# A two-block decoder layer stack: output weights as 512-row by 512-column blocks, and high and low rows side by side in the gate and up products

## The reference

```python
# first block
h = rms_norm(x, norm_mix)
m = gate_0 * (o_sb @ w_sb) + gate_1 * (o_nsa @ w_nsa) + gate_2 * (o_hgrn @ w_hgrn)   # three kinds of attention
x = x + m @ w_out                                    # <- mixer output, 1024 x 1024
x = x + peer_ffn(rms_norm(x, norm_ffn))              # queries, top-16 of keys, 128 gathered expert rows per token
x = rms_norm(x, norm_final)

# second block, two layers
for layer in range(2):
    x = x + 0.5 * rms_norm(swiglu(rms_norm(x), gate, up, down))      # <- F = 2816
    if layer == 0:
        gate_b, gate_c, u = split(rms_norm(x) @ w_conv_in)
        m = (gate_b * conv3(gate_c * u)) @ w_conv_out                # <- convolution output, 1024 x 1024
    else:
        m = diff_attention(rms_norm(x), k, v)
    x = x + rms_norm(m)
    x = x + 0.5 * rms_norm(swiglu(rms_norm(x), gate, up, down))      # <-
    if layer == 0: k, v = split(rms_norm(x) @ w_kv)

swiglu(h) = (silu(h @ w_gate) * (h @ w_up)) @ w_down
```

## Time and profile before

| | us |
|---|---|
| Median of 3 runs (lowest, highest) | 2050.97 (2048.59, 2053.64) |
| Profiled execution, and its span | 2049.09, 2047.2 |
| TensorE matmul busy | 1875.5 (92%) |
| VectorE busy | 1271.8 (62%) |
| ScalarE busy | 773.6 (38%) |
| POOL busy | 409.6 (20%) |
| Mean granted TensorE clock | 0.962 of full speed |

### The profile page before, as it was taken

The page is one execution under the profiler, slowest core; times in us unless marked ns, Lnnn a source line. Parts: engine busy times, 40 slices in busy tenths (PEclk is TensorE's granted clock), DMA queues, the critical chain, the costliest instruction groups (busy, mean ns, idle before and its releaser), DMA issues.

```text
span 2047.2 us, 30706 instructions
## 1 busy us (share of the span) xinstructions
PE 1875.5 (92%) x11294; PEld 1507.1 (74%) x11294; DVE 1271.8 (62%) x2508; ACT 773.6 (38%) x1293; POOL 409.6 (20%) x523
## 2 busy tenths in 40 slices
PE   7999999987877887878889999999999999899998
PEld 7999899943333333333369999999989999778997
DVE  4546856777777767777654457664455545676444
ACT  4446334222222222222243344453345334565333
POOL 4000000345554655555510000000000000010000
PEclk9989999999888888889999999999999999899999
DMA  8324355599999999999966564645555656424553
GB/s 234 102 66 124 83 155 165 224 417 422 422 422 422 422 421 422 422 422 422 421 221 203 184 205 155 197 163 184 185 171 169 205 184 205 144 93 155 185 185 102
DMA packets 228343, 496.73 MB, mean 243 GB/s; under 512 B 21653, under 2 KB 178470, under 8 KB 195494
## 3 DMA queue, kind: packets, MB, share of 16 engines
q1 hardware_dynamic: 185360, 221.36, 34.3%
q0 software_dynamic: 38224, 273.04, 32.4%
q10 hardware_dynamic: 4678, 1.21, 0.3%
HBM read 494.53 MB, written 1.05 MB: 242 GB/s over the span
## 4 chain that ended last, share of the span: by engine, by line
PE 69%; DMA 15%; DVE 6%; POOL 4%; issue 3%; ACT 2%; DVEq 0%; POOLq 0%; ACTq 0%
PE ps L2186 43%; PE acc L2186 25%; DMA rows_xl<-in_peer_uv,idx_now 14%; POOL rows_lo L726 1%; DMA rows_lo<-in_peer_uv,idx_now 1%; POOL rows_xh L726 1%; DVE lo L1387 1%; DVE arena L1774 0%; DVE arena L1778 0%; DVE arena L1781 0%; POOL idx_now L719 0%; DVE arena L1603 0%; ACT diag L1085 0%; POOL rstd L641 0%; ACT arena L1166 0%
## 5 line engine op out<-in xcount | busy, mean ns | idle before, releaser
L1387 DVE TENSOR_TENSOR lo<-raw,hi 128x2048 fp32r<-128x2048 f32 x198 | 451.6, 2283 | 307.7 <-ACT hi L784 307.6
L2186 PE MATMUL ps<-xh,hi 128*128 128x256 f32 x1840 | 524.9, 285 | 2.6 <-DVE xl L1408 2.1
L2186 PE MATMUL ps<-xl,hi 128*128 128x256 f32 x1840 | 522.5, 284 | 0.0
L2186 PE MATMUL ps<-xh,lo 128*128 128x256 f32 x1840 | 522.4, 284 | 0.0
L784 ACT ACTIVATE hi<-raw 128x2048 fp32r<-128x2048 f32 x198 | 376.4, 1904 | 256.4 <-PE ps L2186 230.4
L2186 PEld LDWEIGHTS ps<-xh,hi 128*128 128x128 f32 x1840 | 354.1, 192 | 6.0 <-issue 4.4
L2186 PEld LDWEIGHTS ps<-xl,hi 128*128 128x128 f32 x1840 | 354.2, 192 | 1.5
L2186 PEld LDWEIGHTS ps<-xh,lo 128*128 128x128 f32 x1840 | 354.1, 192 | 0.1
L636 POOL TENSOR_SCALAR ss<-ss 128x1 f32<-128x1 f32 x28 | 9.4, 337 | 1019.2 <-ACT arena L1166 861.7
L2186 PE MATMUL acc<-rows,diag 128*128 128x512 f32 x192 | 116.9, 773 | 73.8 <-ACT diag L1085 72.0
L2186 PE MATMUL acc<-arena,diag 128*128 128x512 f32 x384 | 172.4, 595 | 6.0 <-ACT diag L1085 5.4
(11 more groups left out here) (420 smaller groups left out, 3308.6 us busy)
## 6 DMA issues: line engine op xcount, KB each, us to landing
raw<-in_w_ffn_gate SPq DMA_DIRECT2D x44, 1024.0 KB, 5.4
raw<-in_w_ffn_down SPq DMA_DIRECT2D x44, 1024.0 KB, 4.9
raw<-in_w_ffn_up SPq DMA_DIRECT2D x41, 1024.0 KB, 5.3
raw<-in_w_in SPq DMA_DIRECT2D x29, 1024.0 KB, 5.4
raw<-in_w_conv_in SPq DMA_DIRECT2D x11, 1024.0 KB, 5.2
raw<-in_w_kv SPq DMA_DIRECT2D x6, 1024.0 KB, 5.4
raw<-in_w_out SPq DMA_DIRECT2D x4, 1024.0 KB, 5.2
raw<-in_w_conv_out SPq DMA_DIRECT2D x4, 1024.0 KB, 7.2
```

What stands on the lines that cost most here:

```text
L1387: v.tensor_tensor(lo[s][:, 0:WORDS[p]], raw[s][:, 0:WORDS[p]], hi[s][:, 0:WORDS[p]].bitcast(F32), ALU.subtract).then_inc(lo_done, 1)
L2186: return nc.tensor.matmul(out, l, r, start=first, stop=last)
```

## The change

1. **Gate and up panels of steps 1 to 10.** `xh` and `xl` become two interleaved views of one buffer, so that the high and low rows of a row block lie side by side. `wide` takes high weights against all 512 columns of a row block in one matmul, and low weights against the 256 high columns. The left half of a bank holds high x high and low x high, the right half high x low. A panel so needs two banks (one for each 128 features): gate in 0 and 1, up in 2 and 3. ScalarE copies the right halves out (`cross`), VectorE adds the left halves to them (`gate_sum`, and the first operation of `product`), SiLU and the product then read and write SBUF. The first wide panels wait for the first step's product, and for its turned rows, between their two halves.
2. **`w_out` and `w_conv_out`.** Each is loaded as four blocks of four row blocks by 512 columns (`quarter`): the upper two first, then the lower two. A tile is 12 matmuls of 512 columns. A bank's sum starts in one panel and ends in another. `project` goes. In the mixer output the third panel's split moves up on ScalarE.

```diff
...
-SUM_STEPS = [1 if n == "pc" else 3 for n, _ in POSTS]
+SUM_STEPS = [2 if n == "pc" else 3 for n, _ in POSTS]
...
-        xh = sb("xh", [P, KD, T], F32R)
-        xl = sb("xl", [P, KD, T], F32R)
+        xboth = sb("xboth", [P, KD, 2, T], F32R)
+        xh, xl = xboth[:, :, 0, :], xboth[:, :, 1, :]
...
+        ff_x = [carve(2, T) for _ in range(2)]
...
+        def quarter(w, j):
+            return w[j // 2 * 512:(j // 2 + 1) * 512, j % 2 * 512:(j % 2 + 1) * 512].rearrange("(k p) n -> p k n", p=P)
...
-                load(p, rows_1024(io["w_out"][0], j * PC))
+                load(p, quarter(io["w_out"][0], j))
...
-            split(FIRST["w_out"] + 2)
+                if n == 0:
+                    split(FIRST["w_out"] + 2)
...
+                def cross(p, up, m=0, r=0):
                     act.wait_ge(panel_used, p + m * r + 1)
-                    act.wait_ge(evacuated, along(EVAC, p, m, r))
-                    nc.scalar.activation(ff_s.rearrange("p f t -> p (f t)"), bank(BANK[p]), ACT.Silu).then_inc(evacuated, 1)
-
-                def upper(p, down_done, m=0, r=0, out=ah[:, :, :]):
-                    act.wait_ge(evacuated, along(EVAC, p, m, r) + 2)
+                    act.wait_ge(evacuated, along(EVAC, p, m, r) - 1)
+                    nc.scalar.activation(ff_x[up], PS[:, 2 * up:2 * up + 2, T:2 * T], ACT.Copy).then_inc(ff_cross, 1)
+
+                def silu(p, i, m=0, r=0):
+                    act.wait_ge(evacuated, along(EVAC, p, m, r) + 1)
+                    act.wait_ge(ff_done, FF_STEPS * f + i)
+                    nc.scalar.activation(ff_s, ff_s, ACT.Silu).then_inc(ff_silu, 1)
...
                     split(p0 + 3, 3, i - 1)
+                    cross(p0 + 1, 0, 3, i - 1)
                     split(p0 + 4, 3, i - 1)
-                    silu(p0 + 1, 3, i - 1)
+                    silu(p0 + 1, i, 3, i - 1)
+                    cross(p0 + 2, 1, 3, i - 1)
                     split(p0 + 5, 3, i - 1)
-                    upper(p0 + 1, p0 + 4 + 3 * (i - 1), 3, i - 1)
+                    upper(i, p0 + 4 + 3 * (i - 1))
...
                 i = FF_STEPS - 1
                 split(p0 + 3, 3, i - 1)
+                cross(p0 + 1, 0, 3, i - 1)
                 split(p0 + 4, 3, i - 1)
+                silu(p0 + 1, i, 3, i - 1)
                 if following is not None:
                     split_spare(following)
-                silu(p0 + 1, 3, i - 1)
-                upper(p0 + 1, p0, 3, i - 1, fh)
+                cross(p0 + 2, 1, 3, i - 1)
+                upper(i, p0, fh)
...
+                def gate_sum(i):
+
+                    dve.wait_ge(ff_cross, 2 * ((FF_STEPS - 1) * f + i) - 1)
+                    v.tensor_tensor(ff_s, PS[:, 0:2, 0:T], ff_x[0], ALU.add).then_inc(evacuated, 1)
...
                 def product(p, i, m=0, r=0):
-                    dve.wait_ge(evacuated, along(EVAC, p, m, r))
-                    dve.wait_ge(panel_used, p + m * r + 1)
-                    wait(dve, ff_lo, FF_STEPS * f + i)
-                    v.tensor_tensor(ff_a.rearrange("p f t -> p (f t)"), ff_s.rearrange("p f t -> p (f t)"), bank(BANK[p]), ALU.mult)\
-                        .then_inc(evacuated, 1)
+                    dve.wait_ge(ff_cross, 2 * ((FF_STEPS - 1) * f + i))
+                    v.tensor_tensor(ff_x[1], PS[:, 2:4, 0:T], ff_x[1], ALU.add).then_inc(evacuated, 1)
+                    dve.wait_ge(evacuated, along(EVAC, p, m, r) + 1)
+                    dve.wait_ge(ff_silu, (FF_STEPS - 1) * f + i)
+                    dve.wait_ge(ff_lo, FF_STEPS * f + i)
+                    v.tensor_tensor(ff_a, ff_s, ff_x[1], ALU.mult).then_inc(ff_done, 1)
...
                     split(p0 + 3, 3, i - 1)
+                    gate_sum(i)
                     split(p0 + 4, 3, i - 1)
                     product(p0 + 2, i, 3, i - 1)
                     split(p0 + 5, 3, i - 1)
                     rest(i)
...
+            def quarter_tile(p, j, t, out, lh, ll, ks=range(KD // 2)):
+
+                wh, wl = views(p, KD // 2)
+                r = slice(t * P, (t + 1) * P)
+                for k in ks:
+                    d = j // 2 * (KD // 2) + k
+                    last = exact3(out, lh[:, d, r], ll[:, d, r], wh[:, k, :], wl[:, k, :], d == 0, d == KD - 1)
+                return last
...
+            def out_tile(j, t, ks=range(KD // 2)):
+
+                if not t:
+                    begin(w0 + j)
+                for k in ks:
+                    pe.wait_ge(m_lo, (1, 1, 2, 3)[(j // 2 * 4 + k) // 2])
+                    last = quarter_tile(w0 + j, j, t, bank(2 * t + j % 2), xh, xl, (k,))
+                return last
...
+            out_tile(0, 0)
+            out_tile(1, 0)
             out_tile(0, 1).then_inc(panel_used, 1)
+            for j in (2, 3):
+                out_tile(j, 0).then_inc(out_summed, 1)
+            out_tile(1, 1).then_inc(panel_used, 1)
             turn_rows(0, 0)
-            out_tile(1, 1, range(0, 2))
+            out_tile(2, 1, (0,))
             turn_rows(0, 1)
-            out_tile(1, 1, range(2, 4))
+            out_tile(2, 1, (1,))
             pe.wait_ge(x_added, HALVES)
             query(0, 0)
-            out_tile(1, 1, range(4, 6))
+            out_tile(2, 1, (2,))
             first_scores(0)
-            out_tile(1, 1, range(6, 8)).then_inc(panel_used, 1)
-            out_tile(2, 1).then_inc(panel_used, 1)
+            out_tile(2, 1, (3,)).then_inc(panel_used, 1)
             out_tile(3, 1).then_inc(panel_used, 1)
...
+                def wide(p, up, m=0, r=0, second=None):
+
+                    begin(p, m, r)
+                    wh, wl = views(p, KD)
+                    for h in range(2):
+                        if h and second:
+                            pe.wait_ge(*second)
+                        out, c = bank(2 * up + h), slice(h * P, (h + 1) * P)
+                        for k in range(KD):
+                            both = xboth[:, k, :, :].rearrange("p a t -> p (a t)")
+                            if k < KD - 1:
+                                mm(out, wh[:, k, c], both, k == 0, False)
+                                mm(out[:, 0:T], wl[:, k, c], xh[:, k, :], False, False)
+                            else:
+                                mm(out[:, 0:T], wl[:, k, c], xh[:, k, :], False, False)
+                                last = mm(out, wh[:, k, c], both, False, True)
+                    last.then_inc(panel_used, 1)
...
-                panel_a(p0 + 1)
-                pe.wait_ge(evacuated, EVAC[p0] + 2)
+                pe.wait_ge(evacuated, EVAC[p0 + 1])
+                wide(p0 + 1, 0, second=(ff_done, FF_STEPS * f + 1))
+                pe.wait_ge(ff_done, FF_STEPS * f + 1)
                 rows = ff_a.rearrange("p f t -> p (f t)")
                 for j in range(2):
                     for t in range(TT):
                         last = nc.tensor.transpose(bank(3)[:, j * T + t * P:j * T + (t + 1) * P],
                                                    rows[:, t * PC + j * P:t * PC + (j + 1) * P], ident[:, :])
                 last.then_inc(ff_turned, 1)
-                panel_a(p0 + 2)
+                wide(p0 + 2, 1, second=(ff_lo, FF_STEPS * f + 1))
                 down(p0 + 3, 0, first=True)
                 with pe.Fori(2, FF_STEPS - 1) as i:
-                    panel_a(p0 + 1, 3, i - 1)
-                    panel_a(p0 + 2, 3, i - 1)
+                    wide(p0 + 1, 0, 3, i - 1)
+                    wide(p0 + 2, 1, 3, i - 1)
...
+            def conv_out_tile(j, t):
+
+                begin(p0 + j)
+                for k in range(KD // 2):
+                    pe.wait_ge(cv_lo, (j // 2 * 4 + k) // 2 + 1)
+                    last = quarter_tile(p0 + j, j, t, ACC[:, 2 * t + j % 2, :], yh, yl, (k,))
+                return last
+
+            for j in range(2):
+                conv_out_tile(j, 0)
+                conv_out_tile(j, 1).then_inc(panel_used, 1)
+            for j in (2, 3):
+                conv_out_tile(j, 0).then_inc(sum_ready, 1)
+            for j in (2, 3):
+                conv_out_tile(j, 1).then_inc(panel_used, 1)
...
```

More of the change, by code:

```diff
@@ L87, in ffn @@
     def ffn(name):
-        add(name, 1, spare=1)
+        add(name, 1)
         for _ in range(1, FF_STEPS):
@@ L298, in build @@
         rows += [over(f"rows_{w}{s}", [P, ROW], f"{w}{s}")[:, :] for w in ("hi", "lo") for s in late]
-        rows += [over(f"rows_{w}", [P, ROW], w)[:, :] for w in ("xh", "xl")]
+        rows += [over(f"rows_x{j}", [P, ROW], "xboth", 4 * ROW * j)[:, :] for j in range(2)]
         rows += [raw[late[1]][:, :], home[4], home[5], home[0]]
@@ L588, in _ @@
             for j in range(4):
-                load(FIRST["conv_out"] + j, rows_1024(io["w_conv_out_2"][0], j * PC))
+                load(FIRST["conv_out"] + j, quarter(io["w_conv_out_2"][0], j))
             load_ffn(1, SPARE["ffn1"], kv_cols(1, 1))
@@ L1131, in ffn @@
                 split(p0 + 1)
-                silu(p0)
+                act.wait_ge(panel_used, p0 + 1)
```

(38 more changed lines are left out.)

25 lines of the change are left out of this document (9 added, 16 removed).

## The result

| | before | after |
|---|---|---|
| Median of 5 runs each (lowest, highest) | 2050.97 (2048.59, 2053.64) | 2039.21 (2038.44, 2041.31) |
| Profiled execution, and its span | 2049.09, 2047.2 | 2039.77, 2037.9 |

After to before: 0.9941, 95% interval 0.9929 to 0.9952. That is 11.8 us faster by the medians, where 14.9 were forecast (2036.1), and 9.3 by the two profiled executions. (For the kernel before, the table ahead of the prediction has three runs and this one five; the median is the same.) A second measurement of both kernels gave 2040.33 against 2051.88, 0.9944.

The account below looks back on a forecast made before the run. TensorE's back-to-back matmuls were taken to bound the feed-forward passes. Terms -15.2 + 5.6 - 3.0 - 2.3 = -14.9 us, applied to the median 2051.0, gave 2036.1 us; range 2030 to 2046.

Parts of the forecast that it names:

- (a): Rival: waits at the four pass ends drop the clock, four times 4.9 us, giving 2041; chance 0.08.
- (b): Rival: the mixer output's lead is lost because gathers or buffers set the expert stage, giving 2039.1; chance 0.10.
- (c): Rival: in the wide panels removing a matmul saves nothing, a pair costs 0.360, giving 2051.3; chance 0.08.
- (d): Rival: in the mixed stream the narrow matmul's weight load cannot hide; pair at 0.370 gives 2064; chance 0.06 with (e).
- (e): Rival: within the feed-forward loop a late split takes over; priced with (d), chance 0.06 together.
- part 1: Wide gate and up panels in 10 later steps of 4 passes: 0.19 us saved on each of 80, -15.2 us.
- the prediction's lower bound: In part 1, 512-column matmuls always at 0.232: panel 5.63 us, 0.13 saved per panel, -10.4 us.
- Pass ends: Copy and sum lengthen the last chain: wait grows 1.5 us in ffn0 to ffn2, 1.1 in ffn3; together +5.6 us.
- Mixer output: Three tiles need only row blocks 0 to 3, hiding the wait for merged rows: -3.0 us (bounds 0 and -3.5).
- Convolution output: Four tiles need only early rows; a wait of 1.2 us remains: -2.3 us (bounds -1.5 and -3.5).
- Cover in the loop: Added copies and sums fit idle time within a feed-forward step: cost 0; 1.4 us a step if cover were gone.
- Start of a pass: First half of the first wide gate panel, 2.78 us, covers the 1.95 us turn chain: cost 0, up to 0.5 a pass.

Follow-up runs that it names:

- the fourth run: Changed kernel with matmuls of a whole panel of two halves grouped by width (14 wide, 16 narrow, 2 wide) where nothing is waited for between them: 2033.89 us, 0.9912.
- all-wide run: Changed kernel with the low weights too run against all 512 columns, so all 32 matmuls of a wide panel are 512 wide: 2164.83 us.
- grouped runs: Changed kernel with wide and narrow matmuls grouped instead of alternating: within each half 2035.46 us, over the whole panel of two halves 2033.89 us.
- the seventh run: Changed kernel with only the spare panel's split moved ahead of the gate copy in the last step of a pass: 2035.96 us, one run.
- the third to the ninth run: Edits of the changed kernel: widths grouped (two runs), all matmuls wide, pass ends (two runs), mixer split put back, grouping plus pass ends; 2026.92 to 2164.83 us.

## Why the prediction was right, and where it was off

**Direction, range and mechanism: right.** 2039.2 lies in 2030 to 2046, 3.1 above the forecast. That the median came so near is in part luck: the profiled executions differ by only 9.3 us, and the ledger below accounts for no more. No rival took place. (a) No clock drop at the pass ends: the windows there read 1.00, and the matmuls behind 1.58 us of idling stand 0.227 to 0.236 apart from the second on. (b) The mixer's lead is kept: the gather starts 3.7 us earlier, the first transpose of ffn0 3.4. (c) A removed matmul does save something: 7.5 ns in the changed kernel (9.6 us for 1280), 12 where each width runs in a block (the fourth run). The all-wide run has 0.2267 us for a matmul of 512 columns, 213 ns and 13 on top. The Trainium skill (TensorE: Matmul & The Clock Gate, Back-to-back issue gap) has 2.5 on top, for the isolated gap; in these streams the measurement decides. (d) No pair near 0.364. (e) No idle TensorE in the loop.

**The step that was mis-sized: the price of a pair, in part 1.** I had two readings of the same down panel, 0.232 for the first six wide matmuls behind narrow ones and 0.227 for the rest, and took their mean, 0.228, "since a whole down panel, entry included, cost 0.228 per matmul". But in a stream that alternates, no wide matmul ever gets past the first few behind a narrow one. A panel cost 5.64 us instead of 5.57, and the two panels of a step 11.27 instead of 11.51: 0.24 less, 9.6 us in 40 steps where 15.2 were forecast. Another 0.8 came back, which I had not counted: a down panel takes 5.447 instead of 5.467. Behind the alternating stream only its first matmul costs more (0.233), behind a narrow stream the first five do; why is open. Together 10.4 against 15.2. The step of 16.72 us lies above the 16.55 to 16.65 that I had named as the sign.

The total of a pair, 0.352, is the prediction's lower bound, 0.232 + 0.120, but the agreement to the last digit is luck. In the three pairs above a wide one costs 0.236 and a narrow one 0.117. The bound's sum also had a slip: 5.755 less 5.63 is 0.12 a panel and not 0.13, 9.8 us and not 10.4.

The grouped runs confirm the step from the other side. Behind narrow matmuls the wide ones stand 0.233, 0.236, 0.228, 0.233 and 0.231 apart and then 0.227 (so it is five that cost more, not six); that makes 1.84 us for eight and 3.65 for sixteen, as measured. In return the first narrow one behind wide ones costs 0.114.

**The other terms.**
- Pass ends: forecast +1.5 in three and 1.1 in ffn3, +5.6. The waits grew by 1.41 three times and are 0.90 at the last, and the 48 matmuls around them take 1.37, 1.37, 1.39 and 1.12 us longer: +5.3. The chain was the one described, the spare panel's split included (the seventh run).
- Mixer output: forecast -3.0. From the wait near 134 us to the first index 252.21 before, 249.17 after: -3.0. Window clock 1.00 and no idle time but 0.09 us, as said.
- Convolution output: forecast -2.3 with a wait of 1.2. From ffn0's first transposes to ffn1's turned rows it is 2.2 shorter in the run with the blocks alone, and the wait is 1.07.
- Cover in the loop: forecast 0, and right; even the step of 16.57 us shows no idle time.
- Start of a pass: forecast 0, up to 0.5. The turn was in time, but ffn0 shows two waits of 0.19 and 0.40 us for the splits of its first panels, about 0.6 us, in ffn0 only. That they belong to the change is not shown. ScalarE had idled 6.68 us there for the load of the up weight; in the second trace of the kernel before it idled 6.75, and TensorE waited 0.32 for such a split. With the wide panels alone there was no such wait in one trace and one of 0.22 in the other.

**The ledger of the two profiled executions.** First stretch -0.7, mixer -3.0, expert stage +0.3, start of ffn0 +0.6, steps -10.4, pass ends +5.3, convolution -2.2, differential attention +0.4, start of ffn3 +0.4: -9.3, as in the spans. The two stretches that grew by 0.4 are alike: TensorE idles there for about 3 us, and behind it narrow matmuls stand 0.213 us apart, the pace of the 1.2 GHz level, for a while that differs from trace to trace. At the start of ffn3 that was from 1850.6 to 1853.8 in the kernel before, and from 1842.3 to 1846.1 in the changed one, whose transposes ahead of it ran at half pace too (granted clock 0.50 from 1840 to 1846). The start of ffn3 took 10.68 and 10.69 us in the two traces of the kernel before, 11.07 and 10.98 in the changed one, 11.15 with the blocks alone, 10.66 and 10.70 with the wide panels alone, and 10.47 to 10.68 in the third to the ninth run; the stretch in the differential attention scatters likewise, from 17.45 to 18.74. So these 0.8 us follow neither part of the change, and I take them for chance. The medians say 11.8, since the profiled execution of before lay 1.9 under its median and that of after 0.6 above.

## What to carry to other kernels

Where a price depends on what stands next to the instruction, take the reading with the same neighbours, not the mean over a stream: the first few rows behind a change came nearer here, and the mean hid them. When matmuls of two widths share a bank, try each width in a block: here it took 0.11 to 0.15 us off a step of 16.72. At the end of a pass each instruction on the chain shows in full, so put work that nobody waits for yet (the split of a spare panel) ahead of it.

## What the runs showed of the hardware

The first five wide matmuls behind narrow ones cost 1 to 9 ns more than 0.227 us, 26 in all (0.233, 0.236, 0.228, 0.233, 0.231; the grouped runs and the kernel before), and the first narrow one behind wide ones 6 less than 0.120. Where the widths alternated, a wide one cost 0.236 and a narrow one 0.117 in the mean. It did not depend on the operand's layout (the all-wide run). The same distances, 0.236, 0.228, 0.233 and 0.231, stand behind the wait of 1.58 us at the end of ffn0, where all matmuls are wide, after a first one of 0.307. So it is not the width alone that brings them. They do not follow every wait: behind that of 0.90 us in ffn3 the first is 0.310 and the rest 0.227. What keeps count of this is not visible in the traces; the weight loads run beside the matmuls in either order.

In the first stretch, narrow matmuls stood 0.21 us apart, the pace of the 1.2 GHz level, from 16.3 to 20.9 us in the kernel before; in the changed kernel they start 0.12 apart, are at 0.21 only from 17.0 to 20.0, and then 0.12 again. Over all traces 22 to 26 distances are of that length without the blocks and 14 to 16 with them. Eight of them at 0.213 in place of 0.120 are the 0.7 us. The granted clock reads 1.00 from 17 to 19 us in the kernel before and 0.50 in the changed one, although the distances between starts are the same there, so that column alone is not to be trusted so early in the execution. Why the blocks alter it was not tried.
